# Forget-gate page attention: who requests the pages of the cache

## What is computed

```python
def gather_pages(pool, page_table):
    g = pool[page_table]
    return g.reshape((g.shape[0], g.shape[1] * g.shape[2]) + g.shape[3:])

def fox_attention(q, q_pos, k, v, logf):
    c = jnp.cumsum(logf.astype(F32), axis=1)
    c_k = c.reshape(B, L, G, R).transpose(0, 2, 3, 1)
    def block_fn(qb, pos):
        qg = qb.reshape(B, Q, G, R, D).astype(F32) * (D ** -0.5)
        c_q = c[:, pos].reshape(B, Q, G, R, 1)
        s = jnp.einsum('bqgrd,blgd->bqgrl', qg, kf) + (c_q - c_k[:, None])
        p, _ = masked_softmax(s, (kpos[None, :] <= pos[:, None])[None, :, None, None, :])
        return (jnp.einsum('bqgrl,blgd->bqgrd', p, vf).reshape(B, Q, H, D),)

def odd_layer(x, norm_g, w_in, b_f, w_out, past):
    ...
        kv_all = jnp.concatenate([past[0], kv_new], axis=1)
    o = fox_attention(q, q_pos, kv_all[:, :, 0], kv_all[:, :, 1], lf_all)
```

## Time and profile before

| What | Value |
|---|---|
| median of 3 runs | 3611.28 us |
| the profiled execution, its own time | 3590.15 us |
| its span, first to last instruction | 3588.3 us |
| granted TensorE clock, mean of the span | 0.921 |
| PE busy | 3189.9 us, 89% |
| POOL busy | 596.9 us, 17% |
| stage `s_fox`, first block | about 2954 to 2982 us of the span |
| stage `s_fox`, second block | about 2982 to 3418 us of the span |

### The profile page before, as it was taken

How to read it: one execution, slowest core, us unless ns; L and a number is a source line. 1 busy time by engine, 2 the same in 40 slices (tenths; PEclk the granted TensorE clock), 3 DMA queues, 4 the chain that set the end, 5 groups by cost and what they waited for, 6 DMA issues and landing times. The chain is left out here.

```text
span 3588.3 us, 66202 instructions
## 1 busy us (share of the span) xinstructions
PE 3189.9 (89%) x22697; PEld 2105.6 (59%) x22697; DVE 1459.8 (41%) x4164; ACT 988.7 (28%) x2334; POOL 596.9 (17%) x953
## 2 busy tenths in 40 slices
PE   8999997999999898998767768899978878999968
PEld 4355446988888655565435544466645655666633
DVE  3100101444444245555345548322147664555522
ACT  1000000323323255566113321100035542344311
POOL 0000002222221000000114535100011112333200
PEclk9989998999999779998687979999989998999979
DMA  5533555444443132223468966434132208999751
GB/s 183 203 124 129 181 199 135 136 123 124 122 123 90 35 90 59 81 60 93 142 225 279 302 197 234 156 123 144 43 88 66 67 23 298 336 329 338 254 199 73
DMA packets 331488, 556.73 MB, mean 155 GB/s; under 512 B 70930, under 2 KB 213466, under 8 KB 327482
## 3 DMA queue, kind: packets, MB, share of 16 engines
q1 hardware_dynamic: 252212, 346.29, 30.4%
q0 software_dynamic: 54256, 174.12, 15.1%
q10 hardware_dynamic: 24700, 32.09, 2.6%
HBM read 490.59 MB, written 118.25 MB: 170 GB/s over the span
## 5 line engine op out<-in xcount | busy, mean ns | idle before, releaser
L344 PE MATMUL PS<-even_w,even_xT 128*128 128x512 f32 (+1 forms) x1152 | 491.7, 586 | 2.0 <-DMA even_w<-in_w_in_e 2.0
L1222 PE MATMUL PS<-cmp_xT,cmp_w 128*128 128x255 f32 (+2 forms) x2176 | 487.2, 375 | 1.1 <-DVEq L1302 1.1
L1222 PEld LDWEIGHTS PS<-cmp_xT,cmp_w 128*128 128x128 f32 x2176 | 393.7, 191 | 47.6 <-issue 1.2
L1109 ACT ACTIVATE cmp_xT<-PS 64x512 f32<-64x512 f32 x260 | 154.8, 596 | 930.4 <-PE PS L1193 928.8
L344 PEld LDWEIGHTS PS<-even_w,even_xT 128*128 128x128 f32 x1152 | 220.8, 194 | 254.7 <-issue 248.8
L1109 DVE COPY cmp_xT<-PS 64x512 f32<-64x512 f32 x260 | 179.3, 690 | 290.2 <-PE PS L1193 288.3
L344 PE MATMUL PS<-odd_w,odd_xT 128*128 128x368 f32 x896 | 289.2, 479 | 1.4 <-DVE odd_xT L293 1.4
L300 DVE COPY even_o<-PS 128x512 f32<-128x512 f32 (+3 forms) x81 | 50.3, 622 | 441.4 <-PE PS L344 427.5
L344 PEld LDWEIGHTS PS<-odd_w,odd_xT 128*128 128x128 f32 x896 | 169.0, 193 | 100.4 <-issue 5.4
L1128 POOL DMA_DIRECT2D cmp_pairs<-in_cache_nsa x256 | 151.5, 599 | 388.0 <-issue 388.0
L1852 POOL DMA_DIRECT2D s_fox_kv<-in_cache_fox x256 | 137.5, 537 | 284.0 <-issue 265.1
(11 more groups left out here) (451 smaller groups left out, 4677.5 us busy)
## 6 DMA issues: line engine op xcount, KB each, us to landing
s_fox_kv<-in_cache_fox SPq DMA_DIRECT2D x256, 256.0 KB, 7.3
s_fox_kv<-in_cache_fox POOLq DMA_DIRECT2D x256, 256.0 KB, 6.9
cmp_pairs<-in_cache_nsa SPq DMA_DIRECT2D x256, 128.0 KB, 2.9
cmp_pairs<-in_cache_nsa POOLq DMA_DIRECT2D x256, 128.0 KB, 3.0
s_sel_kv<-in_cache_nsa POOLq DMA_DIRECT2D x256, 128.0 KB, 4.5
s_sel_kv<-in_cache_nsa SPq DMA_DIRECT2D x256, 128.0 KB, 4.6
out_dil_sample<-in_cache_dil_w SPq DMA_DIRECT2D x8, 4088.0 KB
even_w<-in_w_in_e SPq DMA_DIRECT2D x8, 2048.0 KB, 8.2
```

Source lines behind the costliest of these rows:

```text
L344: last = nc.tensor.matmul(bank(c, t, 128)[:, 0:n], xT[:, k, t * 128:t * 128 + 128], w[:, c % WS, k, 0:n], start=(k == 0), stop=(k == KT - 1))
L1109: last = nc.vector.tensor_copy(dst, x) if l else nc.scalar.activation(dst, x, ACT.Copy)
L1222: last = nc.tensor.matmul(hidden_ps(x, NK)[:, g], w1[:, kv, c, :], xT[:, u % 2, kv, g, c % 8, at:at + NK], start=(c == 0), stop=(c == 15))
```

## The change

In `s_fox` alone SP requests every round and POOL none. In the first block SP loads round 1 right behind round 0, ahead of `fold`, `hsel` and the decay rows. In the second block SP loads rounds 2, 3, 4 ... 63 in turn, with the decay rows at the same rounds as before. POOL keeps its clearing of buffers. Rounds, tiles, waits on `valued`, and all instructions of the other engines are as before; `s_sel` is as before.

```diff
                     load(sp, 0)
                     if fox:
+                        load(sp, 1)
                         sp.dma_start(fold[:], E.c_fold).then_inc(c_in, 16)
...
                     for r in range(1, FIRST, 2):
-                        load(pool, r)
+                        if not fox:
+                            load(pool, r)
...
-                for r in range(FIRST, NR, 2):
+                for r in range(FIRST, NR, 1 if fox else 2):
                     if fox and r % RB == US // 4 and 2 <= r // RB + 1 < DEC_BATCH:
                         load_decay(sp, r // RB + 1)
                     load(sp, r)
 
             @block.gpsimd
             def _(pool):
-                for r in range(FIRST + 1, NR, 2):
-                    load(pool, r)
+                if not fox:
+                    for r in range(FIRST + 1, NR, 2):
+                        load(pool, r)
```

## The result

The kernel before takes 3609.3 us (median of 4 runs), the changed one 3710.51: a ratio of 1.0267, 95% interval 1.0231 to 1.0303. It is slower, by about 101 us where I had forecast 37, and it lies above the range.

A forecast was written before the change was run, and what follows sets the result against it. PE bounds the kernel before, SP after: 62 rounds at 6.9 us plus 15.6 us of decay rows put the last `scores` 37 us later, so 3611.3 + 37 = 3648 us, range 3614 to 3685.

The forecast's parts named there:

- The bound: Main loop of the forgetting stage: PE sets the pace before, 6.28 us a round; after the change SP becomes the bound.
- 62 s - 390.7: Loss in us over SP's 62 second-block rounds at s us each: +37 forecast, zero at s = 6.30.
- the price of 6.9: SP's time per loop round in us: 2.4 to the first page, eight DMAs 4.45, 0.05 to the next round.
- The first block: Loading round 1 on SP adds some 7 us, covered by SP's 13.9 us wait for PE at block end: costs nothing.
- The 7.49 that was set aside: SP's mean time per loop round in the kernel before, 7.49 us; as the price it would give +74 us.
- The issue stays hidden: Rival: SP's loop rounds cost 6.15 us or less, PE stays the bound, 3607 to 3611 us; chance 15%.
- A single queue backs up: Rival: SP's loop rounds cost above 7.5 us, 7.7 from layer 0's paged stage, loss 87 us, 3698; chance 10%.
- The signs: Loop profile after: table reads every 6.9 us, DMA near 305 GB/s, PE's page waits about 35 us, SP's nearly none.

The follow-up runs named there:

- the two kernels that give rounds back to POOL: Changed kernel, but POOL requests every sixth round (3654.99 us) or two of every six rounds (3619.38 us), SP the others.
- four rounds per read: Changed kernel, but SP reads the page numbers of four rounds at once (one pointer read, 32 numbers): 3601.42 us, 0.9973 of the kernel before.
- the one with the first page eight times: Changed kernel, but the eight DMAs of a round all fetch the first of its eight pages: 3681.29 us.
- two reads together: Changed kernel, but each round reads its page numbers in two goes of four, each with a pointer read, both ahead of the eight DMAs: 3777.88 us.
- one round of six on POOL: Changed kernel, but POOL requests every sixth round (5, 11, ... 59) and SP the others: 3654.99 us, 1.0134 of the kernel before.

## Why the prediction was right in its direction and wrong in its size

**The bound: right.** SP's waits were gone, PE waited for pages, the DMA engines emptied between rounds, and the sum 62 s - 390.7 turns the price that was measured into the loss that was measured, to within 5 us. Of those, 3.6 stand at the end: I let the last `scores` follow the last issue by 4 + 2.06 us, and it followed by 9.63 (3497.55 to 3507.18), since PE still had a merge (3.76 us) ahead of the last rounds.

**The step that failed: the pointer read in the price of 6.9.** I put 2.4 us on the time to the first page, "from 1.09 + 1.07 and a quarter", because I expected the reads nearer their medians and floors on a system that is less full. The numbers did that (a mean of 0.94), and the eight DMAs came at 4.36, where I said 4.45. The pointer read came at a mean of 2.05. That is +0.96, less 0.13 and 0.09: 0.74, close to the 0.79 between 6.9 and 7.69. So one read, 62 times over, is more than the missing 49 us (62 x 0.79), and the other two terms took a little of it back. A warning stood in the trace of before. There 28 of 31 rounds waited for PE first, so their reads stood behind a pause, and the 1.09 of the earlier trace rows is the price of such a read. The three without a pause took 1.17 and 4.09 us behind decay rows and 1.05 behind pages, too few and too far apart to give a price. I took a median over reads of one kind for a kernel in which all are of the other. That the pause had made them cheap fits the two kernels that give rounds back to POOL and have both kinds behind pages: with a pause 1.05 (4 reads) and 1.08 us (14) at the median, without one 2.01 (41) and 1.55 (20). No run puts in a pause and nothing else. Rounds 3 to 5 of the changed kernel, which have no wait in the code, took 2.68, 2.19 and 3.01 us, so the dear read is not a hidden wait for PE; this is round 3:

```profile
L1848 SPq TENSOR_LOAD <-in_page_table_ptr x1: 2684/2684/2684, 3011.3 to 3011.3; - x1
```

**The first block: right.** From its first read to the first read of the second block it takes 29.1 us (2975.8 to 3004.9), before 28.4; the cover was 13.9 us and now is 7.5, half as said:

```profile
SPq L1874 <- PEq L1874: 7.5, 1, 7.5
```

That part was not tried alone.

**The 7.49 that was set aside.** The mean price of before would have given +74, nearer to the 90.8 than the 6.9 that I took, but for other reasons than those that came true: in it the pointer read has a mean of 1.28 us, the numbers 1.30 and the eight DMAs 4.61. It would have been luck.

**The issue stays hidden: wrong.** It needed a price of 6.30 or less, and only four rounds per read came there. The Trainium skill, "DMA: Bandwidth & Descriptors", section "Issuing engines are not separate DMA queues", which spoke for it, has two halves. That requests of several engines end on the same 16 DMA engines agrees with this case: one queue moved 337 GB/s, two 332. That the issue time saved is usually small beside the DMA does not: here a round costs SP 7.69 us, and its 2.10 MB take 6.2 at those 337 GB/s.

**A single queue backs up: its price was right, its mechanism not.** 7.7 us was worked out from layer 0's reads and pages and hit the measured 7.69 by luck, as two errors cancel. It has 2.4 us for the reads with their gaps, where 3.3 were measured, and 5.3 for eight pages at 0.66, where 4.36 were; the 0.66 was too dear because medians of the reads were taken off a mean, and layer 0's own DMAs take 0.58 a page. And the mark that I set for it, 7 us and more to land, is not there, 4.3. The queue did not back up.

**The signs.** Table reads every 7.9 us with the decay rows in (484.6 / 61), not 6.9; 270 GB/s in the loop, not 305; PE's waits for pages 49.6 us, not 35:

```profile
DMA packets 75509, 134.12 MB, mean 270 GB/s; under 512 B 8808, under 2 KB 12163, under 8 KB 75437
...
q1 hardware_dynamic: 74957, 133.05, 85.2%
```

The waits for pages alone do not add up to the loss, and I had not said where the rest goes. Another 18.8 us are waits for ACT's copies of the transposed keys, which were 0.7 us before; that pages which come one by one leave no other work between is my reading of it, and no run tries it. And 28.8 us are PE's longer busy time, in part at the lower clock. These two do not lengthen the loop by more than the 5 us that the formula misses, as it has no term for them: SP sets the end, and by that a quicker PE would have waited longer for pages.

## What to carry to other kernels

A median of an instruction's time is that of the place in which it stands; before using it for a kernel in which the instruction stands elsewhere, split it by what stands directly ahead (here, behind a pause or behind DMAs). When work moves from two issuing engines to one, add up the receiver's whole stream, reads and all, against the pace of the engine that bounds, and look for the waits that it will lose. A register read that serves more transfers can buy back what the loss of a second queue costs: four rounds per read made one engine as good as two here.

## What the hardware showed that was not expected

A register read of 4, 8, 16 and 32 page numbers takes 0.48, 0.90, 1.74 and 3.57 us at the median: about 0.11 us a number, with hardly a fixed part, each right behind a pointer read, while that read costs 0.83 us where no DMA stands ahead of it and 0.90 to 0.98 behind pages with half the rows or half the bytes.

Right behind eight pages of 128 rows of 2 KB, on an engine that never pauses, the same read takes about 2 us. How this depends on the queue is odd, and its cause stays open. Take for each read when the last page ahead of it lands, counted from the read's start. In the changed kernel and the one with the first page eight times the reads average 2.2 to 2.5 us where that is 4 to 6 us, but 1.1 in the four reads where it is over 7. With four rounds per read it is over 6 in most and the read is quick, except one of 3.73 us. So far a deep queue looks quick. But with two reads together the three reads at 6 to 7 us take 2.73 to 3.57, and with one round of six on POOL the 15 reads at over 7 average 2.0 and go up to 4.89, so the depth of the queue alone does not tell it either. That it is a matter of the pages' addresses, of the row count alone or of the bytes in flight alone is excluded by the runs; what it is, no run here shows.

Pages written as 64 rows of 4 KB to 64 partitions move at 262 GB/s with the queue's share at 102.2%, and each DMA instruction takes 0.468 us; as 128 rows of 2 KB to 128 partitions they move at 337 with the share at 98.9%, at 0.333 us.
